# A two-layer hybrid decoder step: cache values and gate columns loaded and multiplied in turn, sixteen gates kept, low parts of the merged rows on VectorE

## The reference, cut to what matters

```python
D_MODEL = 1024; SEQ = 256; DEC_BATCH = 8; DEC_SEQ = 4; PAST_LEN = 2048
ATT_GROUPS = ((128, 1), (512, 4), (2048, 16))         # window, dilation; 8 heads of 64 in each group

z = rmsnorm(x, norm_attn) @ w_in                       # 1024 -> 512 u + 3*1536 q,k,v + 2*1024 gates
u, q, k, v, gates = project(...)                       # q and k normalised per head

def band_attention_sample(q, k_all, v_all, n_past, dil, band, slopes):
    idx = n_past + jnp.arange(t)[:, None] - j[None, :] * dil
    kg, vg = k_all[:, idx], v_all[:, idx]              # cached keys and values, then this step's
    sc = jnp.einsum('bthd,btjhd->bhtj', q, kg) * (HEAD_DIM ** -0.5) - slopes * (j * dil)
    lse = jax.nn.logsumexp(sc, axis=-1)
    o = jnp.einsum('bhtj,btjhd->bthd', jnp.exp(sc - lse[..., None]), vg)
    return o, lse.transpose(0, 2, 1)

def merge_branches(pool_o, att_o, gates, w_bp, w_ba, w_o):
    g = jax.nn.sigmoid(gates)
    h = g[..., 0, :] * (pool_o @ w_bp) + g[..., 1, :] * (att_o @ w_ba)
    return h @ w_o

x = x + merge_branches(pool_branch(u), combine_groups(att), gates, ...)
x = x + ffn(rmsnorm(x, norm_ffn))
```

## Time and profile before

| | us |
|---|---|
| median of three runs | 2132.34 |
| lowest, highest | 2131.42, 2133.36 |
| the profiled execution | 2137.59 |
| its span, first to last instruction | 2135.2 |
| PE busy | 2005.6 (94%) |
| DVE busy | 611.2 (29%) |
| ACT busy | 494.2 (23%) |
| POOL busy | 157.2 (7%) |
| mean granted clock of TensorE | 0.951 of full |

### The profile page before, as it was taken

One profiled execution on the slowest core, in us unless ns is written; L12 is line 12 of the kernel. 1 busy time (PEld: TensorE's weight loads), 2 busy tenths in 40 slices (PEclk: granted clock), 3 DMA queues, 4 the chain that ended last, 5 costly groups with the idle time before them and its releaser, 6 DMA issues.

```text
span 2135.2 us, 45458 instructions
## 1 busy us (share of the span) xinstructions
PE 2005.6 (94%) x20817; PEld 1361.2 (64%) x20818; DVE 611.2 (29%) x1017; ACT 494.2 (23%) x753; POOL 157.2 (7%) x237
## 2 busy tenths in 40 slices
PE   6998986989999999996998999999999999999997
PEld 6987844989999998772997444353535343443534
DVE  4455422454444454631344101011100101010111
ACT  3434412343433442621332100000000000000000
POOL 0113100102210010300010000000000000000000
PEclk9999987989999999996998999999999999999998
DMA  7433688444545443479523899999999999999995
GB/s 238 154 126 116 196 310 265 143 134 139 170 166 169 139 146 133 128 251 338 167 67 138 297 377 367 386 366 383 386 363 390 368 386 372 382 367 385 363 385 201
DMA packets 211588, 552.68 MB, mean 259 GB/s; under 512 B 11220, under 2 KB 107516, under 8 KB 194866
## 3 DMA queue, kind: packets, MB, share of 16 engines
q1 hardware_dynamic: 207184, 541.67, 70.3%
q0 software_dynamic: 3072, 8.00, 1.0%
q10 hardware_dynamic: 1138, 0.06, 0.0%
HBM read 542.28 MB, written 7.76 MB: 258 GB/s over the span
## 4 chain that ended last, share of the span: by engine, by line
PE 90%; DMA 3%; DVE 3%; ACT 2%; issue 1%; POOL 1%; SPq 0%; DVEq 0%; ACTq 0%; POOLq 0%
PE psum L819 83%; PE psum L827 7%; DMA low_part<-in_cache_kv_g 1%; DMA low_part<-in_w_in 1%; ACT w_split L1352 1%; DVE w_split L1609 1%; DMA out_kv_prompt<-high_part 0%; DMA high_part<-in_const_a 0%; POOL merged_split L2168 0%; DVE high_part L1602 0%; DVE high_part L1616 0%; DVE branch_split L1838 0%; DVE low_part L1701 0%; DVE high_part L1706 0%; ACT low_part L1386 0%
## 5 line engine op out<-in xcount | busy, mean ns | idle before, releaser
L819 PE MATMUL psum<-low_part 128*32 128x512 f32 (+3 forms) x6926 | 712.1, 539 | 31.3 <-DMA low_part<-in_cache_kv_g 24.3
L819 PE MATMUL psum<-xn_split,w_split 128*128 128x288 f32 x3744 | 523.8, 301 | 25.9 <-DVE xn_split L1624 14.4
L819 PEld LDWEIGHTS psum<-xn_split,w_split 128*128 128x128 f32 x3744 | 513.0, 192 | 41.3 <-issue 24.9
L819 PEld LDWEIGHTS psum<-low_part 128*32 128x32 f32 (+2 forms) x6926 | 242.6, 116 | 435.8 <-issue 379.6
L819 PE MATMUL psum<-low_part,high_part 128*32 128x256 f32 (+3 forms) x6636 | 355.0, 362 | 8.0 <-POOL high_part L2130 4.9
L1609 DVE TENSOR_TENSOR w_split<-low_part,w_split 128x2048 fp32r<-128x2048 f32 x105 | 241.0, 2295 | 368.5 <-ACT w_split L1352 368.5
L819 PEld LDWEIGHTS psum<-low_part,high_part 128*32 128x32 f32 (+1 forms) x6636 | 220.7, 113 | 134.5 <-issue 23.7
L1352 ACT ACTIVATE w_split<-low_part 128x2048 fp32r<-128x2048 f32 x105 | 201.1, 1915 | 379.6 <-PE psum L819 278.4
L827 PE MATMUL psum<-high_part,low_part 128*128 128x128 f32 (+3 forms) x1001 | 141.0, 287 | 16.6 <-DMA high_part<-in_const_a 9.5
L827 PEld LDWEIGHTS psum<-high_part,low_part 128*128 128x128 f32 (+3 forms) x1001 | 113.0, 144 | 59.5 <-issue 45.5
L1332 ACT ACTIVATE high_part<-psum 128x384 f32<-128x384 f32 (+2 forms) x72 | 35.9, 499 | 468.5 <-PE psum L827 437.1
(11 more groups left out here) (129 smaller groups left out, 848.8 us busy)
## 6 DMA issues: line engine op xcount, KB each, us to landing
low_part<-in_we_down SPq DMA_DIRECT2D x112, 1024.0 KB, 7.8
low_part<-in_cache_kv_g SPq DMA_DIRECT2D x72, 1024.0 KB, 5.5
low_part<-in_we_gate SPq DMA_DIRECT2D x64, 1024.0 KB, 8.2
low_part<-in_we_up SPq DMA_DIRECT2D x64, 1024.0 KB, 7.2
low_part<-in_w_in SPq DMA_DIRECT2D x56, 1024.0 KB, 5.1
low_part<-in_we_gate SPq DMA_DIRECT2D x64, 768.0 KB, 6.8
low_part<-in_we_up SPq DMA_DIRECT2D x64, 768.0 KB, 6.7
low_part<-in_w_dense SPq DMA_DIRECT2D x33, 1024.0 KB, 5.2
```

Source lines behind the costliest of these rows:

```text
L819: signal(e.matmul(out, lhsT, rhs, start=start, stop=stop, skip_group_check=mixed), inc)
```

## The change

The order of the second part of the mixer is written anew. The eight gate chunks, which in the kernel before stood in pairs ahead of each branch chunk, now stand among the value chunks, in the order of the loads and on PE: gate 0, two value chunks, gate 1, three value chunks, and so on by `V_BEHIND = (2, 3, 3, 3, 3, 2, 2, 0)`. The four branch chunks follow, and then w_out. For that all sixteen gate tiles are kept (`gate` has 16 places). The first gate chunk is split while the last cached keys are copied; `cacheT` now lies in the split buffer that this first gate doesn't need. The turning of the second half's probabilities comes behind gate 0, `gather_heads(0)` behind gate 4, `gather_heads(1)` between the two tiles of gate 7. The two branches are split into two separate tensors, the pool branch early. The low parts of `merged` are made by DVE, and PE waits for them slice by slice in the first tile of w_out.

```diff
+V_BEHIND = (2, 3, 3, 3, 3, 2, 2, 0)
+def value_steps():
+    out, v = [], 0
+    for gate, n in enumerate(V_BEHIND):
+        out.append(("G", gate))
+        out += [("V", v + i) for i in range(n)]
+        v += n
+    return out
...
-PT1_AT, EX_AT = 12, 6
+EX0_GATE = 4
...
-        cacheT = [view(ws_at + GW * i, J, 128) for i in range(CACHE_SLOTS)]
-        gate = [view(q_at + T * i, T) for i in range(4)]
-        prod = [view(q_at + T * (4 + i), T) for i in range(4)]
-        merged_split = split_view("merged_split", q_at + 8 * T, 2, KT, T)
-        branch_split = split_view("branch_split", v_at, 2, 2, 4, T)
+        free_half = [(L * NW_LAYER + W_MERGE + 1) % SRING for L in range(LAYERS)]
+        cacheT = [[view(ws_at + 2 * CH * free_half[L] + GW * i, J, 128) for i in range(CACHE_SLOTS)] for L in range(LAYERS)]
+        gate = [view(q_at + T * i, T) for i in range(2 * KT)]
+        prod = [view(q_at + T * (2 * KT + i), T) for i in range(4)]
+        merged_split = [split_view("merged_high", att_at, KT, T), split_view("merged_low", p_at, KT, T)]
+        branch_split = [split_view("pool_branch_split", strips_at + KT * T, 2, 4, T), split_view("att_branch_split", v_at, 2, 4, T)]
...
# PE
+                def gates(n):
+                    w = chunk(L, W_MERGE + n).rearrange("p a (k n) -> p a k n", k=KT)
+                    for x in range(2):
+                        project(S, (f"g{n % 2}", n // 2 * 2 + x), lambda a, k: w[:, a, k, 128 * x:128 * (x + 1)], xn_parts)
+                        if (n, x) == (KT - 1, 0):
+                            gather_heads(1)
+                    done.append(split_used)
+
+                for kind, n in V_STEPS:
+                    if kind == "V":
+                        cache_values(n)
+                        continue
+                    gates(n)
+                    if n == 0:
+                        turn_s_probs(1)
+                    elif n == EX0_GATE:
+                        gather_heads(0)
...
-                    if i == 0:
-                        gather_heads(1)
-                        e.wait_ge(bl_ready.sem, bl_ready.at(L, 2))
+                            if (i, x) == (0, 0):
+                                e.wait_ge(bl_ready.sem, bl_ready.at(L, b + 1))
...
-                e.wait_ge(ml_ready.sem, ml_ready.at(L, KT))
                 for c in range(KT):
                     w = chunk(L, W_OUT + c // 2).rearrange("p a (k n) -> p a k n", k=KT)
-                    project(S, ("wo", c), lambda a, k: w[:, a, k, 128 * (c % 2):128 * (c % 2 + 1)], merged_split)
+                    project(S, ("wo", c), lambda a, k: w[:, a, k, 128 * (c % 2):128 * (c % 2 + 1)], merged_split,
+                            merged=ml_ready.at(L, 0) if c == 0 else None)
...
# ACT
+                    if m == HB * NT - 9:
+                        split_high(L, W_MERGE)
                 sample_exp(e, L, 1)
-                place_probs(e, L, S, 1)
-                split_high(L, W_MERGE)
-                split_high(L, W_MERGE + 1)
+                for n in range(KT):
+                    split_high(L, W_MERGE + n + 1)
+                    for x in range(2):
+                        job = (f"g{n % 2}", n // 2 * 2 + x)
+                        S.wait_full(e, job)
+                        S.freed(e.activation(gate[2 * job[1] + n % 2], S.ps(job)[:, 0:T], ACT.Sigmoid), job)
...
# DVE
+                    if m == HB * NT - 8:
+                        split_low(L, W_MERGE)
...
+                for n in range(KT):
+                    if n == EX0_GATE:
+                        own_columns(0)
+                    if n == KT - 1:
+                        own_columns(1)
+                    split_low(L, W_MERGE + n + 1)
+                    if n == 0:
+                        new_probs(1)
+                    elif n == 3:
+                        branch_low(0, poolT)
+                    elif n == EX0_GATE + 1:
+                        sample_out(0)
+                sample_out(1)
+                branch_low(1, attT)
...
+                        if c >= 2:
+                            merge_low(c - 2)
+                for c in (KT - 2, KT - 1):
+                    merge_low(c)
...
# POOL
-                    if c >= 2:
-                        merge_low(L, c - 2)
-                merge_low(L, KT - 2)
-                merge_low(L, KT - 1)
```

177 lines of the change are left out of this document (84 added, 93 removed).

## The result

The changed kernel takes 2075.24 us (median of four runs, 2075.11 to 2076.95), beside 2132.85 us for the kernel before (four runs, 2131.42 to 2133.89). The ratio is 0.9732, with a 95% interval of 0.9715 to 0.9749: faster by 57.6 us. I had forecast 2064 us, a gain of 68.7. The profiled execution took 2075.19 us, with a span of 2073.4 us (before 2137.59 and 2135.2), at a mean granted clock of 0.972 (before 0.951).

A forecast was written before the change was run, and what follows sets the result against it. PE, busy 94% of the span, was taken as the bound, with time only in its waits and slow stretches. Per layer 129.1 + 6.7 + 3.4 + 1.2 = 140.4 us, together 68.7 us off, forecast 2064 us, range 2046 to 2088.

The forecast's parts named there:

- gates 2, 3 and 5: Sign in the mixer: a wait for the split at these gates of each layer, 1 to 3 us.
- the stretch to the end of w_out: Sign: from gate 0 to the end of w_out, 135 to 142 us at a clock over 0.95.
- the DMA share up to the branches: Sign: DMA share over 0.9 in the stretch from gate 0 up to the last value.
- The waits in the values: Mixer's value chunks: PE's waits for cache chunks fall from 24.3 to under 3 us; no value chunk late.
- The sum of PE's work: Gates to w_out, without a wait: 77.9 us, branches 25.6 and w_out 25.6, together 129.1 us per layer.
- The waits for new gates: Gates among the values: low parts late at gates 2, 3, 5 and 7, 6.7 us per layer, bounds 0 and 9.
- The clock: New-token matmuls: two falls to half clock per layer, 3.4 us; bounds 0 and 13.6.
- The end of the keys: Last key copies: gate 0's early split puts the last scores 1.2 us later; bounds 0 and 4.2.
- The branches and w_out: Behind the gates: the branch's 5.05 us wait goes, the merged rows' 3.83 nearly whole; cost 0, bounds 0 and 1.
- B: Rival: the clock falls at every gate, 13.6 instead of 3.4 us per layer, 2084 us; 21% together with D.
- D: Rival: loads run no better than values alone; keys' end and ring cost 10 us a layer more, 2084; 21% with B.
- C: Rival: each gate becomes load plus split, 16.75 us, deciding from 15.9 per gate on; about 2143 us; 3%.

The follow-up runs named there:

- e2: Changed kernel with gate 0, two value chunks, gate 1, the other sixteen value chunks, then gates 2 to 7 without a value between: 2108.28 us.
- e1: Changed kernel with each gate's load from gate 1 on issued one value chunk earlier, PE's order the same: 2059.90 us.
- e4: Changed kernel with merged's low parts made on POOL again and PE waiting for all eight ahead of w_out: 2085.83 us.
- e7: Changed kernel with gates' loads two value chunks earlier and each value slot given back with the chunk's own last matmul: 2057.97 us.
- e10: Changed kernel with new tokens and two value chunks ahead of gate 0, later gates' loads one value chunk earlier, value slots given back at once: 2056.80 us.
- e3: Changed kernel with the first gate chunk split behind the second half's exponential, not between the last key copies: 2089.48 us.
- e6: Changed kernel with gates' loads one value chunk earlier and each value slot given back with the chunk's own last matmul: 2057.64 us.
- e11: Changed kernel with only the load order edited, each gate's load two value chunks earlier: 2064.68 us.
- e8: Changed kernel with gates' loads one value chunk earlier, value slots given back at once, and values spread as (2, 2, 2, 3, 3, 3, 3, 0): 2064.94 us.
- e9: Changed kernel with the first half's new tokens and two value chunks ahead of gate 0 on PE, gate 0's load still first: 2072.09 us.

## Why the prediction was right, and where it was off

Direction and range were right; the gain came out at 57.6 us where 68.7 were forecast. Of the signs written down, the wait for cache chunks is gone, the waits of the branch and of the merged rows are gone, and gates 2, 3 and 5 wait in both layers, though up to 3.85 us and not 3. Two signs failed: the stretch to the end of w_out is 145.6 and 143.0 us and not 135 to 142, and the DMA share up to the branches is 0.86 and 0.89 and not over 0.9. Step by step:

**The waits in the values.** Right. The 24.3 us for cache chunks are gone, no value chunk waits, and e2 brings them back together with about 33 us.

**The sum of PE's work.** Right: 25.50 us for the branches and 25.62 for w_out against 25.6 each, and the stage without its waits and its lost clock is 94.35 - 12.97 - 4.03 = 77.4 us in layer 0 and the same in layer 1, against 77.9. Its parts were off and cancel: a gate takes 6.5 to 6.6 us start to start and not 6.40, a value chunk 0.93 (2.79 for three) and not 1.06, the new tokens 2.77 and not 2.5, since the window of 5.00 us in the earlier trace rows doesn't hold the whole of them.

**The waits for new gates: the term that was mis-sized.** Forecast 6.7 us per layer, measured 13.0 and 10.5. The mechanism is the one stepped through (gate 2's load needs value chunk 1's slot, which comes free when gate 1 begins), but two of its numbers were too good. I had gate 2's load landing 6.8 us from its issue, with value chunk 4 issued 1.1 us ahead of it. A value slot does not come back when PE starts its next piece, as I stepped it, but when the first matmul of that piece has ended, which for value chunk 1, whose four tiles run side by side, is only near its end; so the slots of value chunks 0 and 1 came back at 298.35 and 298.70, about when gate 1 began (298.30). Both loads were issued then, 0.41 us apart, and gate 2's landed after 8.0. The earlier trace rows had shown that the loads of w_in in this stretch take 12.5 us in the median, and I had set them aside for the shortest of the earlier trace rows: a load that is issued close behind another doesn't take that. The same hand-over repeats at the gates behind: gate 3's load is issued at 311.50, when gate 2 has begun (311.07), and waits of 3.85 at gate 3 and 3.00 at gate 5 stand against 1.7 and 2.8 stepped. Gate 6, which I had stepped as in time, waits 2.73 and 1.58, and gate 7, stepped 0.3 late, doesn't. e1 shows that this, and not a lack of DMA, was the limit: one place in the load order took 7.7 us out of each stage. My upper bound for the term, 9, was too low too: it varied only the speed of a cache chunk, not the time at which a slot comes back.

**The clock.** Forecast 3.4 us per layer, measured 2.55 + 1.48 = 4.0 in layer 0 and 2.46 + 1.45 = 3.9 in layer 1 (what the slow gates take over 6.66). The size came out near and the place wrong, so the size is luck: I had put two falls at the new-token matmuls, where the granted clock stayed at 1.00, and none for certain at the gates. They stand behind waits, of 3.85, 2.73, 3.38 and 2.34 us; behind other waits of like length (3.39 and 3.00) there was none. The number of falls isn't fixed either: in e4, whose stage is the same code, there are three slow gates in each layer, at 8.1 to 8.2 us. Nor can the new tokens be ruled out as a place, as layer 0 of e7 and layer 1 of e10 show. The Trainium skill (TensorE: Matmul & The Clock Gate, section "HAM oscillation — how this bites in real kernels") says of short bursts of matmuls that wait for data between them that each next one starts cold. Taken as a rule for every start behind a wait, it fits the four places, but would have predicted nine. Which waits cost a fall stays open.

**The end of the keys.** Forecast 1.2 us, measured 1.7 (e3), inside the bounds. What was bought with it, the hidden split and softmax, is worth 14.2 us in the whole (e3), more than the 2 x 5.35 us of waits that I had for it: gate 0 also runs slowly behind its wait in e3 (8.35 and 8.34 us for 6.66).

**The branches and w_out.** Right: both waits are gone, and w_out went from 28.43 to 25.62 us. e4 brings the wait and the lower clock back for 10.6 us in the medians, known to some 5 us; 2 x (3.83 + 2.8) = 13.3 would have been the prediction's own figure, and the traces give 2 x 3.83 + 2.27 + 2.42 = 12.4.

**The account.** Gates 2 x 6.7 = 13.4 forecast, 23.5 measured: 10.1 us. Clock 1.1, keys 1.0. PE's own work was 0.5 us shorter in each layer than forecast, so 1.0 the other way. Together 11.2 us less gain than 68.7, so 57.5; the medians say 57.6. An agreement this close is luck, since the terms are known to about 1 us each. The profiled executions differ by 62.4 because that of before stands 4.7 us above its median.

Of the rivals none took place. B would have the clock fall at every gate; it fell at two per layer. D comes nearest: the ring did cost 6.3 and 3.8 us a layer more than I had and the keys 0.5, where D had 10, and the DMA share of 0.86 and 0.89 in the stage is no better than the 0.94 of the values in the kernel before:

```profile
288.83:346.05 57.22, 39.48 (x175) 10.31 (x171) 5.76 (x9) 4.68 (x7) 0.00 (x0) 0.65 0.94 319
```

That the loads stood still for want of a slot, and could run better, e7's share of 0.97 shows. C is excluded by the steps from gate to gate, 311.07 - 298.30 = 12.8 us from gate 1 to gate 2 and at most 14.8 (gate 3 to 4), under the 15.9 from which it decides.

## What to carry to other kernels

When two kinds of loads share a ring of slots, step through it with the time at which each slot is given back, and give a load issued behind another the time of both; a bound that varies only the speed of a load misses the lateness. The order of the loads need not be that of the work: what has to be split or converted after landing should be issued one or two places ahead of what is used in place (7.7 us per stage here, for an edit of a few lines). Several long waits in a row are best read as one shortage: take away the first cause in an experiment and see what is late next.

## What the runs showed that was not expected

The kernel's time varies by 2 us in the changed kernel, but by 12 to 17 in e6, e7 and e11. The traces put part of it ahead of the stage: the way from the first half's probabilities to the end of the keys takes about 18.6 us in most, but in layer 1 it takes 23.25 in e6, 23.08 in e7, 22.44 in e8 and 23.53 in e10, with the clock down at its end. These are the four kernels that have both edits, the early loads and the slot given back at once, and none of the others with early loads or the slot edit alone shows it. With one trace of each, that is a coincidence or an effect of the edits on a place ahead of the stage; the runs don't tell which. A comparison of medians finer than some 5 us between such kernels says little; the stage lengths say more, to the 1.0 to 1.3 us that e4 shows.

Waits of 3.0 to 3.5 us ahead of a gate left the clock at full in four places (3.39 and 3.00 in the changed kernel, 3.21 and 3.41 in e9) and were followed by a slow gate in five (3.38 in the changed kernel, 3.25, 3.35 and 3.37 in e3, 3.30 in e4). What decides between them the runs don't tell, and I did not test it.
